# Another order of the expert kinds, one more full-size expert, and three overflow places instead of four

## What is computed

```python
logits = (xf @ router_w).astype(jnp.float32)
top_val, top_idx = lax.top_k(logits, TOP_K)        # 2 of 8
gates = jax.nn.softmax(top_val, axis=-1)
...
y = swiglu(x_pad[tok_b], w1[e], w3[e], w2[e])      # (silu(x w1) * (x w3)) w2, 1024 -> 3584 -> 1024
y = y * gate;  out = segment_sum(y, token)
```

## Time and profile before

| | |
|---|---|
| median of three runs | 1462.97 us |
| the profiled execution | 1462.97 us, span 1461.2 us |
| PE busy | 1378.0 us (94%) |
| DVE busy | 875.8 us (60%) |
| ACT busy | 704.9 us (48%) |
| GpSimd busy | 45.5 us (3%) |
| read from HBM | 472.46 MB, 324 GB/s over the span |

### The profile page before, as it was taken

How to read it: one execution, slowest core, us unless ns; L and a number is a source line. 1 busy time by engine, 2 the same in 40 slices (tenths; PEclk the granted TensorE clock), 3 DMA queues, 4 the chain that set the end, 5 groups by cost and what they waited for, 6 DMA issues and landing times.

```text
span 1461.2 us, 19216 instructions
## 1 busy us (share of the span) xinstructions
PE 1378.0 (94%) x7838; PEld 1006.0 (69%) x7838; DVE 875.8 (60%) x1181; ACT 704.9 (48%) x983; POOL 45.5 (3%) x65
## 2 busy tenths in 40 slices
PE   6999999999999999999879999879999997999995
PEld 4875899999889977784348884346666434888432
DVE  2478898878885699980049980047676202999101
ACT  3467644434564577761048861036665102887100
POOL 0000000000000000001001001002000100100100
PEclk9999999999999999999999999999999999999999
DMA  9976667887973348999999999999676999999996
GB/s 346 326 283 242 229 246 259 304 293 256 344 277 127 116 158 317 337 342 409 402 409 409 402 384 409 403 409 367 250 268 255 355 405 407 409 404 408 381 405 246
DMA packets 157911, 474.81 MB, mean 325 GB/s; under 512 B 6493, under 2 KB 8682, under 8 KB 157818
## 3 DMA queue, kind: packets, MB, share of 16 engines
q1 hardware_dynamic: 156448, 472.27, 84.6%
q10 hardware_dynamic: 1370, 1.25, 0.3%
HBM read 472.46 MB, written 1.05 MB: 324 GB/s over the span
## 4 chain that ended last, share of the span: by engine, by line
PE 75%; DVE 9%; DMA 9%; SPq 3%; ACT 2%; issue 1%; ACTq 0%; DVEq 0%
PE bank L1562 11%; PE bank L1486 11%; PE bank L1490 10%; PE bank L1489 10%; DMA ring<-in_moe_w 6%; SPq L695 3%; DVE ada_acc L2244 2%; PE bank L1554 2%; PE bank L875 2%; PE bank L838 2%; PE bank L832 2%; PE bank L1407 2%; DMA ring<-in_ffn_w 2%; PE bank L1052 2%; DVE w_lo L2445 2%; PE bank L1054 2%
## 5 line engine op out<-in xcount | busy, mean ns | idle before, releaser
L2795 DVE TENSOR_TENSOR w_lo<-ring,w_hi 128x1024 fp32r<-128x1024 f32 x336 | 406.5, 1243 | 120.8 <-ACT w_hi L1998 111.5
L1998 ACT ACTIVATE w_hi<-ring 128x1024 fp32r<-128x1024 f32 x336 | 354.1, 1063 | 140.7 <-PE bank L1490 103.7
L1562 PE MATMUL bank<-ring,work 128*64 128x512 f32 (+1 forms) x1024 | 199.1, 541 | 14.4 <-DMA ring<-in_moe_w 14.4
L1486 PE MATMUL bank<-w_hi,hg_hi 128*128 128x512 f32 x448 | 180.3, 403 | 12.6 <-DVE w_lo L2795 12.1
L1489 PE MATMUL bank<-w_lo,hg_hi 128*128 128x512 f32 x448 | 177.4, 396 | 0.0
L1490 PE MATMUL bank<-w_hi,hg_lo 128*128 128x512 f32 x448 | 177.3, 396 | 0.0
L2947 DVE TENSOR_TENSOR work<-work,bank 128x512 f32<-128x512 f32 (+1 forms) x16 | 9.9, 622 | 270.7 <-PE bank L1562 270.7
L1562 PEld LDWEIGHTS bank<-ring,work 128*64 128x64 f32 x1024 | 78.7, 137 | 125.7 <-issue 116.1
L1554 PE MATMUL bank<-ring,work 128*64 128x512 f32 x448 | 102.8, 597 | 22.7 <-DMA ring<-in_moe_w 22.7
L1486 PEld LDWEIGHTS bank<-w_hi,hg_hi 128*128 128x128 f32 x448 | 86.1, 192 | 40.6 <-DVE w_lo L2795 19.9
L2244 DVE SCALAR_TENSOR_TENSOR ada_acc<-ring,c_act,ada_acc 128x512 f32<-128x512 f32 x140 | 105.0, 750 | 3.9
(11 more groups left out here) (461 smaller groups left out, 2247.4 us busy)
## 6 DMA issues: line engine op xcount, KB each, us to landing
ring<-in_moe_w SPq DMA_DIRECT2D x168, 2048.0 KB, 13.9
ring<-in_ada_w SPq DMA_DIRECT2D x24, 2048.0 KB, 12.7
ring<-in_ffn_w SPq DMA_DIRECT2D x15, 2048.0 KB, 8.2
ring<-in_gla_w_in SPq DMA_DIRECT2D x6, 2048.0 KB, 12.9
ring<-in_da_w_in SPq DMA_DIRECT2D x4, 2048.0 KB, 12.6
ring<-in_da_w_in SPq DMA_DIRECT2D x4, 1024.0 KB, 17.6
ring<-in_da_w_out SPq DMA_DIRECT2D x2, 2048.0 KB, 10.6
ring<-in_gla_w_out SPq DMA_DIRECT2D x2, 2048.0 KB, 11.2
```

What stands on the lines that cost most here:

```text
L1486: begun = mm(out[:, :], xhi, whi[:, cs], start=first, stop=False)
L1562: last = mm(psum[0 if what == "w1" else 6][h * HALF:(h + 1) * HALF, 0:hw], xb[:, k, :], w[:, kk, h * hw:(h + 1) * hw], start=(k == 0), sto ...
L1998: A(w_hi[:, moe_slot(Q), :], raw_piece(SPLITS[r], q), ACT.Copy).then_inc(hi_done, 1)
L2795: v.tensor_tensor(w_lo[:, moe_slot(Q), :], raw_piece(SPLITS[r], q), w_hi[:, moe_slot(Q), :].bitcast(F32), ALU.subtract).then_inc(lo_done, 1)
```

## The change

Position by position, the kinds go from A B A B C B A B to A B C B A A A B. So there are three B passes where there were four, and four A passes where there were three. `PLACES` goes along with it: the fullest of the sorted experts (rank 0) stays with C, ranks 1, 2 and 3 get the A's of positions 4, 5 and 6 (ranks 1 and 2 had them), and ranks 4, 5 and 6 stay with B's. `OVER` goes from 4 to 3, and the branch of the fourth overflow pass goes on the three engines.

```diff
-OVER = 4
+OVER = 3
...
-BASE = "ABABCBAB"
+BASE = "ABCBAAAB"
...
-PLACES = (NE - 1, 3, 1, 4, 0, 5, 2, 6)
+PLACES = (NE - 1, 4, 0, 5, 1, 2, 3, 6)
...
                     with pe.If(more[2] == 2):
                         overflow(2)
-                        with pe.If(more[3] == 2):
-                            overflow(3)
```

More of the change, by code:

```diff
@@ L2189, in _ @@
                         overflow(2)
-                        with act.If(more[3] == 2):
-                            overflow(3)
             store_end()
@@ L2984, in _ @@
                         overflow(2)
-                        with dve.If(more[3] == 2):
-                            overflow(3)
 INPUTS = ["x", "c", "ada_w", "ada_b", "norm1_g", "norm2_g", "da_w_in", "da_q_gain", "da_k_gain", "da_lam_q1",
```

## The result

The changed kernel takes 1488.57 us, the median of four runs (1485.81 to 1491.12), against 1463.47 us for the kernel before (1462.1 to 1464.12). The ratio is 1.0172, with an interval of 1.0152 to 1.0193: it is slower, by 25.1 us between the medians. The profiled execution took 1490.64 us with a span of 1488.9 us.

The account below looks back on a forecast made before the run. PE was taken to bound an A, weight loads a B, and loading nearly an A with its B. Two A's at 243.3 + 1.0 + 0.2 - 218.95 gave +25.6 us on 1462.97, so 1488.6 us, range 1484 to 1496.

Parts of the forecast that it names:

- Loads set an A with the B behind it: Expert part: an A and the next B together cost 218.95 us, nearly two experts' loading, 218.0 us at 404 GB/s.
- No overflow pass: Expert routing: 336 weight splits are four experts of 84, so no overflow pass ran and none can be saved or added.
- (1): Start of an A behind an A: no wait and no half-clock start on PE, saving 2.6 us each.
- (2): Position 5: its A gathers no tokens, saving 3.5 us; the A's at 5 and 6 take 120.0 and 123.3 us.
- (3): Borders from A to A: DVE may be late with split pieces; 0.5 us of PE waiting each, 1.0 in all.
- (4): Last B, now behind an A with a full ring: taken as 0, between -9.4 and +2.4 us.
- (5): Small parts: gather of 256 columns at position 4 adds 0.2 us; moved copies and one overflow place fewer taken as 0.
- (a): Rival, A's behind an A: DVE falls behind by 4.8 us each as in the first A, 1497.2 us; chance 0.12.
- (b): Rival, last B: the full ring lets it run 5 us shorter, 1483.6 us; chance 0.06.
- (c): Rival, positions 5 and 6: loading alone sets an A behind an A, 215.4 us for two, 1459.4 us; chance 0.02.
- (d): Rival, adjacent A's: loading slows to 358 GB/s or so and holds other experts alike, about 1463 us; chance 0.02.
- (e): Rival, routing: an overflow pass ran or will run, costing or saving at least 114 us; chance 0.02.

Follow-up runs that it names:

- e2: Kernel before, with the third matmul of each piece (tokens' low part by weights' high part) left out in A and C passes; 1420.71 us, ratio 0.9713.
- e7: Kernel before with three overflow places instead of four (OVER = 3) alone, same order of kinds; 1462.66 us, ratio 0.9995.
- e8: Changed kernel, with the two DVE products that take out an A's result done three times over at positions 5 and 6; 1494.59 us, one run.
- e1: Changed kernel with the same kinds in the order AAABCBAB, two A's behind an A at positions 1 and 2; 1489.92 us, ratio 1.0182.
- e3: Changed kernel, with the third matmul of each piece left out in A and C passes; 1421.20 us, ratio 0.9715 to the kernel before.
- e4: Kernel before, with idle matmuls in the B's ahead of an A or C, 3 before the last slot and 8 behind; 1471.78 us, ratio 1.0073.
- e5: Kernel before, with fewer idle matmuls in those B's, 1 before the last slot and 4 behind; 1461.29 us, ratio 0.9984.

## Why the prediction was right

The time was forecast as 1488.6 us and measured as 1488.57. Of the difference of 25.6 us by the sum, the medians show 25.1 and the expert part of the profiles 25.04. The mechanism held, but agreement to 0.1 us is luck: the sum is 0.5 us too high, and the median of before rose by as much, from 1462.97 to 1463.47 us. Inside the sum, 1.0 us of lag that didn't come is offset in part by 0.5 us more in A5 and A6.

- **Loads set an A with the B behind it.** Held: shown by e2, where A2 shrank by 11.4 us and the pair by 1.4.
- **No overflow pass.** Held: the split stands 420 times, five experts of 84.
- **(1) and (2), the A behind an A.** Forecast before any lag: 120.0 and 123.3; measured 120.04 and 123.75. Both the lost slow start and the missing gather came out; the trace shows no wait at the border. The gather was put at 3.5 us, while its own rows give 3.6 (two passes of 1.71 and 0.08 behind each), and A6 took 3.7 longer than A5. That the slow start cost 2.6 us was one execution's: e7's had 7 slow matmuls and not 12, some 1.7 us. The build doesn't hang on it, since e7's A2 is shorter by about as much.
- **(3), DVE's lag.** The term was 1.0 us and the trace shows none at all in A5. The mechanism was the right one to look at: e8 turns 2.9 us more of DVE into an A5 that is 2.9 us longer. The reserve at piece 7 was under-estimated, as the walk had DVE fall behind by its full busy times, while rows on DVE overlap a little (two products 1.28 us, and the next starts 1.20 after the first). The lag beside GpSimd's adds, from which the 0.5 us of each A came, gave no wait either, though the adds took longer (10.16 us) than in A2.
- **(4), the last B.** 0 was taken, +0.24 measured.
- **(5), small parts.** C2 came out 0.6 us longer, B3 0.7 shorter (together 0.1 shorter), A4 0.3 to 0.5 longer, A0 0.24 shorter; e7 puts the last down to the shorter table. The gather at position 4 took 1.91 us a pass with 256 columns, against 1.71 with 64, 0.4 us more for the two passes, less 0.16 for the slower first matmul that only a pass of 64 columns has behind it: about the 0.2 forecast. The others are of the size by which the same stretch differs between executions (C4 170.93 before, 170.15 in e7), much of which is the length of the slow start: the first 21 matmul distances of C4 took 7.31 us before and 6.53 in e7.
- **The rivals.** (a), a DVE lag as in A0, is excluded by the waits, and e1 shows that it doesn't come behind A0 either. (b) isn't seen. (c) fails as the A's are at PE's pace; e3 shows it comes near to true once PE has a third less to do: then the order costs 0.5 us. (d): the loads beside the A's did run at 366 and 359 GB/s, but as PE let go of slots late: in e3, with PE relieved, the same two ran at 407 and 394, and B1 kept its 403 in the changed kernel. (e): the split stands 420 times.

The Trainium skill (TensorE: Matmul & The Clock Gate, "Wait — 56ns, not 53.3ns?") gives 215.7 ns from start to start for a warm matmul of 512 columns; by an estimate from that figure A5's 504 matmuls would have taken 5.6 us less. The trace of the changed kernel doesn't agree and decides: A5 took what 0.227 us each gives.

## What to carry to other kernels

Cut a program at its stages and name each stage with what goes ahead of it; if the stages come out the same in every place, a new order can be summed up from the old trace, and only the new neighbours have to be built. A stage that computes longer than it loads is free only next to one that loads longer than it computes, and one such neighbour pays for one of them (e1); how much a deeper or shallower ring would change was not tried. An engine kept busy to hold its clock must end when the data is there: a filler 3.9 us too long (e4) cost more than the clock gave.

## What the runs showed of the hardware

- PE's slow level after a wait of 3.7 us lasted 10 to 12 matmuls of 0.43 us in the profile of before and 7 in that of e7, for the same instructions. In e7 it began only behind two (A2) and six (A6) distances of 0.23 to 0.34 us.
- A matmul on float32 constants with 512 columns took 0.82 us in e4 with the granted clock at 1.00, a 512-column one on rounded operands 0.227 (A5).
- GpSimd's four adds were busy for 6.96 us in A2 of before, 10.16 in A5 of after and 10.47 in A2 of e5, for the same instructions; DVE's splits beside them took 1.65 us in A2, against a mean of 1.25.
